# Three tiles abreast behind each norm, and an on-chip memory map on multiples of 2048 bytes, in a two-layer trunk kernel

## The reference

```python
h = modulate(rms_norm(x, norm_mix), sh_m, sc_m)
(qa, ka, va, qb, kb, vb, qkv_c, z_c, beta_c, a_c, gate) = jnp.split(h @ w_in, IN_OFFSETS, axis=-1)
...
x = x + gt_m * merge_branches(o_a, o_b, o_c, gate, w_branch, w_out)
x = x + gt_f * sq_relu_mlp(modulate(rms_norm(x, norm_ffn), sh_f, sc_f), w_ffn1, w_ffn2)
```

## Time and profile before

| | us |
|---|---|
| median of 3 runs | 3197.92 (3194.75 to 3206.76) |
| the profiled execution, its own time | 3194.49 |
| its span in the profile | 3192.7 |
| PE busy | 2967.9 (93%) |
| DVE, ACT, POOL busy | 1254.3, 1059.5, 1042.4 |
| mean granted TensorE clock | 0.969 |

### The profile page before, as it was taken

The page is one execution under the profiler, slowest core; times in us unless marked ns, Lnnn a source line. Parts: engine busy times, 40 slices in busy tenths (PEclk is TensorE's granted clock), DMA queues, the critical chain, the costliest instruction groups (busy, mean ns, idle before and its releaser), DMA issues.

```text
span 3192.7 us, 57461 instructions
## 1 busy us (share of the span) xinstructions
PE 2967.9 (93%) x24851; PEld 2489.5 (78%) x24851; DVE 1254.3 (39%) x1795; ACT 1059.5 (33%) x1770; POOL 1042.4 (33%) x704
## 2 busy tenths in 40 slices
PE   5998898998789999899999989999999899989998
PEld 3887787786578887688888867788787688768886
DVE  4774343245641113322222268654245611232223
ACT  3542222225542122322221235533225532333222
POOL 2234344220313333122223222355430344434442
PEclk7999999999999999899999989999999999999999
DMA  6116353110002232122222221100320034323331
GB/s 234 53 30 202 134 187 114 53 47 1 11 24 66 63 102 64 45 61 66 60 67 61 66 74 52 48 3 4 85 60 1 11 93 135 97 79 93 99 93 66
DMA packets 303691, 231.94 MB, mean 73 GB/s; under 512 B 16784, under 2 KB 275280, under 8 KB 302544
## 3 DMA queue, kind: packets, MB, share of 16 engines
q1 hardware_dynamic: 297360, 204.58, 21.4%
q0 software_dynamic: 3776, 17.91, 1.5%
q10 hardware_dynamic: 2304, 5.77, 0.5%
HBM read 217.22 MB, written 11.98 MB: 72 GB/s over the span
## 4 chain that ended last, share of the span: by engine, by line
PE 81%; DVE 9%; issue 4%; ACT 3%; DMA 1%; POOL 1%; ACTq 0%; DVEq 0%; POOLq 0%
PE ps L427 21%; PE ps L428 21%; PE ps L429 21%; PE ps L558 5%; PE ps L512 2%; DVE stat L1356 2%; PE ps L533 2%; PE ps L439 1%; PE ps L550 1%; DVE R L1470 1%; PE ps L773 1%; PE ps L723 1%; DVE ps L1353 1%; ACT R L881 1%; PE ps L579 1%
## 5 line engine op out<-in xcount | busy, mean ns | idle before, releaser
L1741 POOL TENSOR_TENSOR wl<-wring,wh 128x1024 fp32r<-128x1024 f32 (+1 forms) x312 | 723.7, 2322 | 1389.6 <-ACT wh L1012 1387.3
L427 PE MATMUL ps<-hh,wh 128*128 128x512 f32 (+1 forms) x2560 | 924.8, 361 | 62.6 <-DVE hl L1331 38.2
L428 PE MATMUL ps<-hl,wh 128*128 128x512 f32 (+1 forms) x2560 | 905.7, 354 | 0.0
L429 PE MATMUL ps<-hh,wl 128*128 128x512 f32 (+1 forms) x2560 | 905.0, 354 | 0.0
L427 PEld LDWEIGHTS ps<-hh,wh 128*128 128x128 f32 x2560 | 491.3, 192 | 155.7 <-issue 44.0
L428 PEld LDWEIGHTS ps<-hl,wh 128*128 128x128 f32 x2560 | 492.2, 192 | 67.7 <-issue 5.1
L429 PEld LDWEIGHTS ps<-hh,wl 128*128 128x128 f32 x2560 | 491.4, 192 | 65.7
L1012 ACT ACTIVATE wh<-wring 128x1024 fp32r<-128x1024 f32 (+1 forms) x312 | 307.7, 987 | 523.7 <-PE ps L429 495.9
L1671 DVE SCALAR_TENSOR_TENSOR R<-ps,modcs,R 128x512 f32<-128x512 f32 x216 | 136.3, 659 | 367.8 <-PE ps L429 366.9
L428 PE MATMUL ps<-fl,wh 128*128 128x512 f32 (+1 forms) x768 | 274.8, 358 | 0.0
L429 PE MATMUL ps<-fh,wl 128*128 128x512 f32 (+1 forms) x768 | 274.5, 357 | 0.0
(11 more groups left out here) (238 smaller groups left out, 3728.8 us busy)
## 6 DMA issues: line engine op xcount, KB each, us to landing
wring<-in_w_ffn SPq DMA_DIRECT2D x128, 512.0 KB, 3.9
wring<-in_w_in SPq DMA_DIRECT2D x116, 512.0 KB, 3.8
wboth<-in_w_mod SPq DMA_DIRECT2D x80, 512.0 KB, 6.3
wring<-in_w_branch SPq DMA_DIRECT2D x48, 256.0 KB, 2.7
wring<-in_w_out SPq DMA_DIRECT2D x16, 512.0 KB, 4.1
x_store<-R POOLq DMA_DIRECT2D x2, 3072.0 KB, 9.0
R<-x_store POOLq DMA_DIRECT2D x2, 3072.0 KB, 11.0
R<-in_w_mod SPq DMA_DIRECT2D x7, 512.0 KB, 13.4
```

What stands on the lines that cost most here:

```text
L427: mm(ps[:, t0:t1], ahk, rh[:, k, t0:t1], start=(k == 0), stop=False)
L428: mm(ps[:, t0:t1], ahk, rl[:, k, t0:t1], start=False, stop=False)
L429: last = mm(ps[:, t0:t1], alk, rh[:, k, t0:t1], start=False, stop=(k == kn - 1))
L1741: G.tensor_tensor(slot_view(wl, n % NSPL, l, name, i), w, slot_view(wh, n % NSPL, l, name, i).bitcast(F32), ALU.subtract)\
```

## The change

It has two parts. The memory map: the constants and small tiles are allocated first, a filler `to_line` takes the memory up to the next multiple of 2048 bytes, and `hh`, `hl`, `wring`, `wh`/`wl` and `R` then each begin on such a multiple. The order behind each norm: a new function `project_three` takes three PSUM tiles at once, waits for steps 0 to 4 one after the other, and at each of them runs that step's products of all three tiles (512 and 256 columns); then it finishes the tiles one by one with steps 5 to 7. For "mix" the three are c4, c5 and `ba`, for "ffn" ff1 0, 1 and 2. Number, shape and operands of the products stay as they are. For their weights, ACT copies the high half of the third tile ahead of the root (ff1 2, and `ba` in the second layer) or right behind it (`ba` in the first), and POOL splits `ba` ahead of the spill.

```diff
+ABREAST = 5
+LINE = 2048
...
+        craw_c = sb("craw_c", [P, 2, KC])
+        base = nc.sbuf_base if not callable(nc.sbuf_base) else nc.sbuf_base()
+        to_line = -((base + 31) // 32 * 32) % LINE // 4
+        if to_line:
+            sb("to_line", [P, to_line])
         hh, hl = (ctx.enter_context(nc.sbuf_tensor(n, [P, KC, TOK], F32R)) for n in ("hh", "hl"))
...
+            def project_three(jobs, ntok, ready):
+
+                homes = [take(pe, *key) for key, _ in jobs]
+
+                def products(i, k):
+
+                    key, (ah, al) = jobs[i]
+                    for t0, t1 in ((0, LAT), (LAT, TOK))[:1 if ntok == LAT else 2]:
+                        to = homes[i][:, t0:t1]
+                        mm(to, ah[:, k, :], hh[:, k, t0:t1], start=(k == 0), stop=False)
+                        mm(to, ah[:, k, :], hl[:, k, t0:t1], start=False, stop=False)
+                        last = mm(to, al[:, k, :], hh[:, k, t0:t1], start=False, stop=(k == KC - 1))
+                    return last
+
+                for k in range(ABREAST):
+                    pe.wait_ge(*ready(k))
+                    for i in range(3):
+                        products(i, k)
+                for i, (key, _) in enumerate(jobs):
+                    for k in range(ABREAST, KC):
+                        if i == 0:
+                            pe.wait_ge(*ready(k))
+                        last = products(i, k)
+                    last.then_inc(*filled(*key))
...
-                for p in range(15):
+                first = [(("c", l, c_order[p]), weights(pe, l, "c", c_order[p])) for p in range(2)]
+                project_three(first + [(("baT", l), weights(pe, l, "ba"))], TOK, lambda k: dve_done.at("h", l, "mix", k))
...
+                        if g == 0:
+                            project_three([(("ff1", l, i), weights(pe, l, "ff1", i)) for i in range(3)], nt,
+                                          lambda k: dve_done.at("h", l, "ffn", k))
...
+                if which == "ffn":
+                    high(l, "ff1", 2, ahead=0)
+                if l and which == "mix":
+                    high(l, "ba", ahead=0)
                 act.wait_ge(*full("ss", l, which))
...
-                    high(l, "c", c_order[0], ahead=1)
+                    high(l, "ba", ahead=0)
...
                 for p in range(2):
                     split(l, "c", c_order[p])
+                split(l, "ba")
                 pool.wait_ge(*dve_done.at("scaled", l, "mix", KC - 1))
                 pool.dma_start(x_store, R[:, XT0:RN]).then_inc(*spilled.mark(l, by=16))
-                split(l, "ba")
```

More of the change, by code:

```diff
@@ L114, in sig @@
             return Signal(nc, ctx, name, book)
+        cst = sb("cst", [P, C_N])
+        pcols = sb("pcols", [P, 2, P])
+        ccol = sb("ccol", [P, KC, 32])
+        modcs = sb("modcs", [P, 2, 48, 2])
+        gains = sb("gains", [P, 2, 2, KC, 2])
+        small = sb("small", [P, 64])
+        eps = sb("eps", [P, 2])
+        bg = sb("bg", [P, TT, 16])
+        gt = sb("gt", [P, TT, 8])
+        gtmp = sb("gtmp", [P, TT, 8])
+        gex = sb("gex", [P, TT, 4, 8])
+        nbeta = sb("nbeta", [P, TT, 8])
+        abc = sb("abc", [P, 2, 8])
+        stat = sb("stat", [P, 8, 2])
+        craw_c = sb("craw_c", [P, 2, KC])
[3 more added lines that the diff above has]
+            sb("to_line", [P, to_line])
         hh, hl = (ctx.enter_context(nc.sbuf_tensor(n, [P, KC, TOK], F32R)) for n in ("hh", "hl"))
@@ L123, in program @@
                   for i, n in enumerate(("wh", "wl")))
[L124 to L130, removed]
         XT0, RN = 21504, 27648
@@ L181, in program @@
         osq = r(6144, TT, 512)
-        bg = sb("bg", [P, TT, 16])
-        gt = sb("gt", [P, TT, 8])
-        gtmp = sb("gtmp", [P, TT, 8])
         gcs = sb("gcs", [P, TT, 32])
-        gex = sb("gex", [P, TT, 4, 8])
-        nbeta = sb("nbeta", [P, TT, 8])
-        abc = sb("abc", [P, 2, 8])
         qk = r(S0, 6, TOK)
@@ L201, in program @@
         eraw = r(S0 + 3072, 2, 8, 32)
-        stat = sb("stat", [P, 8, 2])
         mT = r(S0, KC, TOK)
@@ L206, in program @@
         prow = sb("prow", [P, P])
-        craw_c = sb("craw_c", [P, 2, KC])
         mrow = sb("mrow", [P, P])
@@ L635, in _ @@
                     norm(l, "mix", TOK)
-                for p in range(15):
+                first = [(("c", l, c_order[p]), weights(pe, l, "c", c_order[p])) for p in range(2)]
+                project_three(first + [(("baT", l), weights(pe, l, "ba"))], TOK, lambda k: dve_done.at("h", l, "mix", k))
+                for p in range(2):
+                    slot_read(l, "c", c_order[p], "c", l, c_order[p])
+                slot_read(l, "ba", 0, "baT", l)
+                for p in range(2, 15):
                     if p < 12:
                         j = c_order[p]
-                        project(("c", l, j), weights(pe, l, "c", j), conv_cols(l, j),
-                                ready=(lambda k: dve_done.at("h", l, "mix", k)) if p == 0 else None)
+                        project(("c", l, j), weights(pe, l, "c", j), conv_cols(l, j))
                         slot_read(l, "c", j, "c", l, j)
@@ L645, in _ @@
                         gate_project(l, p - 12)
-                    if p == 1:
-                        project(("baT", l), weights(pe, l, "ba"), TOK)
-                        slot_read(l, "ba", 0, "baT", l)
                     if p == 2:
@@ L837, in _ @@
                     if g < NG:
-                        for i in range(GF * g, GF * g + GF):
-                            project(("ff1", l, i), weights(pe, l, "ff1", i), nt,
-                                    ready=(lambda k: dve_done.at("h", l, "ffn", k)) if i == 0 else None)
+                        if g == 0:
+                            project_three([(("ff1", l, i), weights(pe, l, "ff1", i)) for i in range(3)], nt,
+                                          lambda k: dve_done.at("h", l, "ffn", k))
+                            for i in range(3):
+                                slot_read(l, "ff1", i, "ff1", l, i)
+                        for i in range(max(GF * g, 3), GF * g + GF):
+                            project(("ff1", l, i), weights(pe, l, "ff1", i), nt)
                             slot_read(l, "ff1", i, "ff1", l, i)
```

## The result

The kernel after takes 3164.3 us (median of 4 runs, 3150.9 to 3170.1) where the kernel before takes 3197.7 on the same chip. The ratio is 0.9887, with a 95% interval of 0.9869 to 0.9905. A second series of five runs, further down, gave 3160.0 against 3193.6, ratio 0.9886 [0.9866, 0.9906]. The forecast for the median was 3159.5. The ratios are made from all runs, so they don't match the medians exactly: 0.9887 is 36 us, the medians differ by 33.4.

A forecast was written before the change was run, and what follows sets the result against it. PE holds 81% of the chain, with waits and a low clock behind the norms. Products abreast 27.4 plus map 11.0 give 38.4 us, from 3194.5 to 3156.1, or 3159.5 for the median; range 3150 to 3168, wide 3095 to 3188.

The forecast's parts named there:

- term (a): First layer's first norm: POOL's added third split holds DVE's scaling, so step 0 and all behind come 2.3 us late.
- term (c): Fourth tile's weights, copied only once the first tile completes: PE waits 1.6 us in the fourth norm, some 0.4 in the second.
- I take the gain as kept: Convolution behind "mix": DVE's saturated stretch moves forward with PE's tiles, so the gain there is not given back.
- that holds by little: Behind "mix": c6's copy, split and ACT's small copies end near 87.7, with c6 due at 88.4.
- signs of being wrong: `hh` spacing moved by 5 ns (24 us), PE waits on `wl` behind the third tile, or idle PE between 100 and 230 us.
- rival (3): Gain behind "mix" is given back, the convolution being bound by DVE: 7.4 + 8.9 us lost, 3175.8; chance 0.12.
- Forecast 11.0 us: Memory map: 512-column products with operands in `R` gain 15.8 us, 256-column ones lose 2.2, width changes cost 2.6.
- change of width: Products switching between 512 and 256 columns: the first few steps cost 0.03 us, 2.6 us for 64 + 24 tiles.
- Rival (1): The memory map does nothing: 3170.5 us; chance 0.18.
- rival (2): The map speeds up `hh` too, as each operand's own place counts: floor 3013.5, halfway 3086; chance 0.14.
- Rival (4): New addresses set weights and `hh` against each other worse: 3200.5 or 3236.5 us; chance 0.12.
- first case: `hh` at the pace of `R`, 0.2342: costs 36 us, gives 6 with 256 columns, and loses the map's 11: 3200.5.

The follow-up runs named there:

- experiment 4: Kernel after, with POOL issuing the copy of `xT` to DRAM as soon as `xT` is complete, ahead of the splits: 3161.2 us, ratio 0.9887.
- repeated profile: Profile of the kernel after, run again unchanged in a second series: median 3160.0 us (3157.1 to 3162.8).
- experiment 8: Kernel after, with POOL's copy of `xT` and its three splits issued early, and three steps abreast instead of five: 3149.8 us, ratio 0.9851.
- experiment 1: Kernel before, with the new memory map and nothing of `project_three`: 3185.7 us, ratio 0.9970.
- experiment 3: Kernel after, with `wh`, `wl` and `R` moved 32 bytes further on, so `hh` and `hl` stand off against the weights: 3186.6 us, ratio 0.9966.
- experiment 6: Kernel after, with POOL's three splits of layer 0 ahead of its wait for the parameters: 3157.0 us against 3160.0.

## Why the prediction was right, and where not

**Products abreast.** The mechanism came as forecast: one wait per norm, no gap behind it. The first stretch began 3.2 us later than in the earlier trace rows: 0.95 of it because everything up to the scaling ran later (51.67 for 50.72), and 2.3 by the third split, term (a). For the three tiles, 27.0 us were forecast and 26.7, 27.6 and 28.2 measured; for the fourth norm 20.0 with its wait and 19.8. The clock rose 3.2, 5.0, 3.5 and 3.6 us behind the first product in the first profile and after 5.9, 5.0, 3.5 and 4.4 in the repeated one: 4.3 in the mean, for the 4.4 of the forecast. The wait of 0.4 us in the second norm (term (c)) did not come; one of 1.2 us came in the third, where none was counted.

**The step that failed in part is "I take the gain as kept"**, with "that holds by little" ahead of it. Two of the prediction's own signs of being wrong showed in part. There are waits on `wl` behind the third tile: 1.2 of the 28.2 us of n3 are a wait for the fourth tile's low part, which was gone in experiment 4, where the clearing came earlier (to no profit there, as the clock rose later). And PE is idle for 3.4 us of conv0 (3.6 in the repeated profile) where it was for 1.3. Against before, the repeated profile has conv0 0.9 and conv1 2.1 us longer. That is rival (3), at about 3 of its 16.3 us.

Its cause was another than the forecast and experiment 4 had looked for. At c6, DVE had not given the gain back: its first tap starts at 98.63 for 105.24, 6.6 us earlier, with the third tile's end 6.8 us earlier. But the tap takes 2.75 us where it took 0.62. Before, POOL's two splits fell into DVE's 9.26 us of idle time; now DVE is at work there, and the splits hold it as they hold the first scaling. The rows of POOL before and after:

```profile
97.95 4.75 POOL L1741 TENSOR_TENSOR wl<-wring,wh 128x1024 fp32r<-128x1024 f32 x2 [10.72 <-ACT wh L1012]
```

```profile
94.68 6.28 POOL L1780 TENSOR_TENSOR wl<-wring,wh 128x1024 fp32r<-128x1024 f32 x2 [5.69 <-ACT wh L1051]
```

PE's wait for ACT's square, some 20 us behind the third tile, follows the length of that tap: 1.28 us with a tap of 0.62 (before, and experiment 8), 2.4 with 1.76 (layer 0 of the repeated profile, layer 1 of experiment 4), 3.4 with 2.76 (both layers of the first profile), and in the last case the clock falls too. All convolutions of the profiles with three or five steps abreast have this wait 0.6 to 0.7 us longer than the tap; no run moved these splits alone, so the link is read from the rows and not shown by an experiment of its own. The splits run beside the taps of c5 and end 11.9 us behind the third tile's end in conv1 of the repeated profile, 10.8 in experiment 4 and 6.9 in experiment 8, where c4 ends earlier; the tap starts at 9.6, 9.4 and 9.4. So experiment 4 took back 2.4 us of conv1, and experiment 8 has the tap free again and both convolutions a little shorter than before (147.7 and 124.9). How many us of the 3 are due to this against the kernel before is less sure, as there is one profile of it, and the map alone, with the same tap and the same wait, has conv1 2.9 us longer.

**The map.** Forecast 11.0 us; alone, the ratio says 9.6, the medians and the parts of the table with operands in `R` 12.2. Term by term it holds: a group of twelve `fh` products took 2.75 us, which is 12 x 0.2267 and the 0.03 that the forecast puts on a change of width. From the means over all products at the full clock (`fh` 6.5 ns shorter with 512 columns and 2.3 longer with 256, `ohi` 5.9 and 2.7), it is 13.4 - 2.5 = 10.9 us. Rival (1) falls by experiment 1, rival (2) by the unchanged pace of `hh` in both. Rival (4) did not come about; experiment 3 makes its first case, without the 11 us of the map, and 22 to 27 us were measured for its 30. The rule of the Trainium skill ("TensorE: Matmul & The Clock Gate", Part 2) that loading weights takes nothing from the running matmul does not hold to the nanosecond here: 32 bytes between the operands cost 5.4 ns a product. That the two reads get in each other's way is the nearest reading of this, and no more than a reading.

**The sum.** Repeated profile against before: prologue +1.2, the four stretches -8.7, -9.5, -7.9, -1.3, convolutions +0.9 and +2.1, the parts with operands in `R` -11.0, the delta rule -0.4 (287.1 and 203.0 for 286.3 and 204.3). That makes -34.6 us for the forecast -38.4; the medians say -33.4 and -33.6, the ratios -36. What is missing are the 3.0 of the convolutions and 1.0 in n3. That the second series ended at 3160.0, half a us from the forecast, is luck: its kernel before was 4 us faster than in the first series, and the gain was some 5 us short. The delta rule, on which nothing was forecast, moves by more than that from run to run.

## What to carry to other kernels

Where an engine waits at each step of a stream and its clock falls with it, give it two or three times the work per step and let it wait once; but take no more steps abreast than are needed to bridge the stream (three steps did as well as five and saved 1.5 us behind the fourth norm, eight gave back 13 to 19 us of some 26), since each step delays the first tile, and with it the next weights and whoever works on that tile. Place the moving and the stationary operands of long fp32r matmuls at equal offsets, and check the spacing of products in the timeline, as no busy share shows it. Look where GpSimd's long instructions fall once VectorE has no idle time left: splits that lay beside a VectorE instruction on on-chip memory held it to their end here, whether it was a scaling of 0.75 us or a tap of 0.62, while VectorE's copies out of PSUM beside the same splits kept their 0.29 us (experiment 6).

## What the hardware showed unexpectedly

- The spacing of products depends on the distance between the two operands' addresses, and differently by width: for `hh`, 0.2276, 0.2333, 0.2333 and 0.2327 us with 512 columns at 0, 32, 64 and 128 bytes, and 0.1199, 0.1187, 0.1144 and 0.1192 with 256 (means over all products at the full clock).
- A wait of PE of 4.19 us in the middle of a feed-forward part was followed by products of 0.63 us, one of 1.50 us was not; in the convolution of the second layer the clock fell with a wait of 3.41 us and stayed up with one of 2.39.
- Three splits back to back held a pair of VectorE instructions of 1.15 us for 8.09, to the end of the last split.
- The delta rule of layer 0, with the same number of instructions, took between 282.1 and 295.4 us.
